# Second block: gate products of the sparse branch issued in pieces between the turns of its attention

## What is computed

```
y_c = dsa_mixer(sq, sk, sv, iq, ik, iw)      # per query block: scores, top-k mask, softmax, weighted values
merged = None
for bi, y in enumerate((y_a, y_b, y_c, y_m)):
    term = jax.nn.sigmoid(u @ w_gate[l, bi]) * (y @ w_branch[l, bi])
    merged = term if merged is None else merged + term
h = h + rms_norm(merged @ w_out[l], norm_mix_post[l])
```

## Time and profile before

| quantity | value |
|---|---|
| median of 3 runs | 2868.74 us |
| profiled execution, its span | 2871.6 us |
| TensorE busy | 2789.8 us (97%) |
| VectorE, ScalarE, POOL busy | 1569.8, 1021.7, 1234.4 us |
| share of the chain that ended last: TensorE | 86% |
| DMA, mean | 68 GB/s |
| attention stage (TensorE) | 1899 to 1983.6 us of the span |
| merge of branch c | 1983.6 to 2093.3 us |

### The profile page before, as it was taken

How to read it: one execution, slowest core, us unless ns; L and a number is a source line. 1 busy time by engine, 2 the same in 40 slices (tenths; PEclk the granted TensorE clock), 3 DMA queues, 4 the chain that set the end, 5 groups by cost and what they waited for, 6 DMA issues and landing times.

```text
span 2871.6 us, 41163 instructions
## 1 busy us (share of the span) xinstructions
PE 2789.8 (97%) x15095; PEld 2247.1 (78%) x15095; DVE 1569.8 (55%) x2437; ACT 1021.7 (36%) x1680; POOL 1234.4 (43%) x960
## 2 busy tenths in 40 slices
PE   7999989999999999999998999989999999999998
PEld 5788778887888887788777888866878888888886
DVE  6444431126255246544488999974156665555655
ACT  4444542333233344333354222144344222222223
POOL 1434312237788641222321343311413766766664
PEclk9999999999999999999999999999999999999999
DMA  6111021213321451211110111100141112112114
GB/s 235 48 34 41 19 89 47 94 59 106 110 59 44 139 212 67 57 36 42 49 32 27 48 46 50 48 25 12 47 174 66 44 44 66 44 44 66 44 60 145
DMA packets 236591, 195.13 MB, mean 68 GB/s; under 512 B 24068, under 2 KB 218301, under 8 KB 232509
## 3 DMA queue, kind: packets, MB, share of 16 engines
q1 hardware_dynamic: 235389, 189.39, 20.7%
q10 hardware_dynamic: 1088, 4.19, 0.4%
HBM read 169.37 MB, written 24.18 MB: 67 GB/s over the span
## 4 chain that ended last, share of the span: by engine, by line
PE 86%; DVE 7%; ACT 2%; issue 2%; POOL 2%; DMA 1%; POOLq 0%; DVEq 0%; ACTq 0%; SPq 0%
PE ps L372 38%; PE ps L4527 13%; PE ps L1684 9%; PE ps L2256 5%; PE ps L1989 3%; PE ps L4477 2%; PE ps L4478 2%; PE ps L4479 2%; PE ps L1095 1%; PE ps L1109 1%; DVE score L3624 1%; PE ps L707 1%; PE ps L3959 1%; DMA x_tok<-in_x 1%; PE ps L3970 1%
## 5 line engine op out<-in xcount | busy, mean ns | idle before, releaser
L355 POOL TENSOR_TENSOR w_lo<-raw,w_hi 128x512 fp32r<-128x512 f32 (+2 forms) x278 | 312.6, 1147 | 741.5 <-ACT w_hi L347 741.5
L372 PE MATMUL ps<-h_hi,w_hi 128*128 128x512 f32 x1472 | 584.5, 397 | 0.0
L372 PE MATMUL ps<-h_hi,w_lo 128*128 128x512 f32 x1472 | 573.8, 390 | 0.0
L372 PE MATMUL ps<-h_lo,w_hi 128*128 128x512 f32 x1472 | 573.5, 390 | 0.0
L372 PEld LDWEIGHTS ps<-h_hi,w_lo 128*128 128x128 f32 x1472 | 276.3, 188 | 59.1
L372 PEld LDWEIGHTS ps<-h_hi,w_hi 128*128 128x128 f32 x1472 | 276.3, 188 | 58.8 <-issue 2.1
L372 PEld LDWEIGHTS ps<-h_lo,w_hi 128*128 128x128 f32 x1472 | 276.6, 188 | 55.8 <-issue 0.5
L347 ACT ACTIVATE w_hi<-raw 128x512 fp32r<-128x512 f32 (+2 forms) x280 | 135.9, 534 | 450.5 <-PE ps L372 439.8
L4380 DVE TENSOR_TENSOR acc<-acc,ps 128x1024 f32<-128x1024 f32 x144 | 169.2, 1213 | 5.7
L3725 DVE MATCH_REPLACE8 score<-best,score 128x384 f32<-128x384 f32 (+2 forms) x192 | 165.8, 876 | 0.0
L3726 DVE MAX8 best<-score 128x8 f32<-128x384 f32 (+2 forms) x192 | 155.7, 878 | 1.1
(11 more groups left out here) (575 smaller groups left out, 6217.6 us busy)
## 6 DMA issues: line engine op xcount, KB each, us to landing
raw<-in_w_in SPq DMA_DIRECT2D x86, 512.0 KB, 3.9
raw<-in_w_ffn_gate_up SPq DMA_DIRECT2D x44, 512.0 KB, 4.8
raw<-in_w_gate SPq DMA_DIRECT2D x32, 512.0 KB, 3.9
d_raw<-in_w_ffn_down SPq DMA_DIRECT2D x20, 512.0 KB, 5.5
acc_pair<-acc_kept SPq DMA_DIRECT2D x8, 1024.0 KB, 4.9
x_kept<-acc SPq DMA_DIRECT2D x16, 512.0 KB, 2.6
acc_kept<-acc_pair SPq DMA_DIRECT2D x7, 1024.0 KB, 3.9
w_ada<-in_w_ada SPq DMA_DIRECT2D x6, 1024.0 KB, 12.7
```

The costliest lines, as they stand in the source:

```text
L355: pool.tensor_tensor(w_lo[:, to, cut], raw[:, s, cut], w_hi[:, to, cut].bitcast(F32), ALU.subtract).then_inc(split.sem, 1)
L372: last = pe.matmul(dst, w[:, slot, k], x(k), start=(k == ks[0] and n == 0), stop=(k == ks[-1] and n == 2))
```

## The change

The 8 gate chunks of branch c move into the attention. A chunk's 48 matmuls are cut into 4 pieces of 12, which makes 32 pieces: two stand between the first scores, the other 30 one behind each turn, except behind turns 5, 11, 17, 23, 29 and 35 of 0 to 35. Two pieces fill one bank (the upper half of `ps[3]`) with half a tile, 512 tokens; ACT then copies it into `acc` (`copy_gate`), and the next half waits for that copy. So `acc` holds the raw gates, and the running sum of the other branches is stored to HBM before (`sum_before`, four stores of 1 MB: three in the first merge, one early in the attention). The attention's result keeps the other half of `ps[3]` only, so the first weigh of block n now waits for the result of block n-1. VectorE's `rest_o` is moved ahead of the next block's `bias_scores`. Behind the attention `merge_kept` takes the place of the merge: SP loads the sum back (4 MB) into the space of `h_lo` once the last gate product has been made, and behind these loads come the branch chunks 2 to 7; ACT makes the Sigmoids in place, TensorE the 96 branch matmuls, VectorE multiplies and adds. Nothing of the computation is left out.

```diff
-        def merge(acc, branches, accumulate, following, beside=None, early=None, residual_gate=None, gate_row=None):
+        def merge(acc, branches, accumulate, following, beside=None, early=None, residual_gate=None, gate_row=None, kept=None):
...
+                    if kept is None:
+                        stream(sp, N, per, merge_source(branches), following,
+                               wide_loads if early or residual_gate is not None else None)
+                    else:
+                        source = merge_source(branches)
+                        for i in range(N):
+                            for m in range(2, per + 2):
+                                if i and m == 6:
+                                    sp.wait_ge(o_evicted.sem, o_evicted.at(0, i, len(adds)))
+                                    sp.wait_ge(sum_kept.sem, sum_kept.at(i - 1))
+                                    tiles_done = slice(KT - 2 * i, KT - 2 * i + 2)
+                                    sp.dma_start(kept[:, tiles_done], acc[:, tiles_done]).then_inc(sum_kept.sem, 16)
+                                load_chunk(sp, m, i, per, source(i, m) if m < per else source(i + 1, m - per) if i + 1 < N else
+                                           following(0, m - per))
...
-            gates, tile_added = ended["gates"], ended["tiles"]
+            gates, tile_added, h_used = ended["gates"], ended["tiles"], ended["h_used"]
...
-                    sum_high(act, rows, acc, tile_added)
+                    sum_high(act, rows, acc, tile_added, h_used)
...
-            return chunk_of(w_in2, m * P + S_Q)
-
-        def sparse_attention(y_hi_t, y_lo_t, score, kv_t, following):
+            return chunk_of(w_in2, m * P + S_Q) if m < 2 else chunk_of(w_gate2[2], ROW_ORDER[m - 2] * P)
+
+        def sparse_attention(y_hi_t, y_lo_t, score, kv_t, acc, kept, following):
...
+            PER = 2 + KT
+            PIECES = 4
+            EARLY_PIECES = 2
...
-                    c = n % 2 * HALF + half * 2 * P
+                    c = n % 2 * 2 * P
                     return ps[3][half * 64:half * 64 + 64, c:c + 2 * P].rearrange("p (t c) -> p t c", c=P)
+
+                def gate_bank():
+                    return ps[3][:, HALF:]
+
+                filled = [x for x in range(len(turns)) if x % 6 != 5]
+
+                def piece_of(x):
+
+                    return EARLY_PIECES + filled.index(x) if x in filled else None
...
                 @block.sync
                 def _(sp):
-                    stream(sp, 1, 2, sparse_source, following)
-
-                gates, terms, added = ended["gates"], ended["terms"], ended["sums"]
+                    for m in range(2, PER + 2):
+                        load_chunk(sp, m, 0, PER, sparse_source(0, m) if m < PER else following(0, m - PER))
+                        if m == 3:
+                            sp.wait_ge(*added)
+                            sp.wait_ge(sum_kept.sem, sum_kept.at(KT // 2 - 1))
+                            sp.dma_start(kept[:, 0:2], acc[:, 0:2]).then_inc(sum_kept.sem, 16)
...
-                    for m in range(2):
-                        rest_chunk(pool, m + 1, 0, 2)
+                    for m in range(PER):
+                        rest_chunk(pool, m + 1, 0, PER, KT if m + 1 < PER else BW // P)
...
+                    def copy_gate(piece):
+                        if piece is None or piece % 2 == 0:
+                            return
+                        n, half = piece // PIECES, piece % PIECES // 2
+                        if half == 0:
+                            act.wait_ge(half_made.sem, half_made.at(n + 1))
+                            if n % 2 == 0:
+                                act.wait_ge(sum_kept.sem, sum_kept.at(n // 2 + 1))
+                        else:
+                            act.wait_ge(used.sem, after(used, 2 + n, 0, PER))
+                        act.activation(acc[:, ROW_ORDER[n], half * HALF:half * HALF + HALF], gate_bank(), ACT.Copy).then_inc(half_copied.sem, 1)
+                        if half:
+                            round_chunk(act, n + 4, 0, PER, KT if n + 4 < PER else BW // P) if n + 4 <= PER else None
+
+                    round_chunk(act, 3, 0, PER)
                     for h in range(H):
                         exps(0, h)
+                        if h % 2 and h // 2 < EARLY_PIECES:
+                            copy_gate(h // 2)
...
+                            if j < b:
+                                copy_gate(piece_of(x))
                         for h in heads:
                             exps(n + 1, h)
+                        copy_gate(piece_of(turns.index((n, b))))
...
                     for n in range(0, TT, 2):
                         normalise(n)
+                        if n >= 1:
+                            rest_o(n - 1)
                         bias_scores(n + 1, (0, 1))
                         bias_scores(n + 1, (2, 3))
-                        if n >= 1:
-                            rest_o(n - 1)
                         normalise(n + 1)
+                        rest_o(n)
                         if n + 2 < TT:
                             bias_scores(n + 2, (0, 1))
-                        rest_o(n)
-                        if n + 2 < TT:
                             bias_scores(n + 2, (2, 3))
                     rest_o(TT - 1)
...
+                    def gate_piece(piece):
+
+                        if piece is None:
+                            return
+                        n, part = piece // PIECES, piece % PIECES
+                        if part == 0:
+                            split_ready(pe, 2 + n, 0, PER)
+                        if part % 2 == 0:
+                            pe.wait_ge(half_copied.sem, half_copied.at(piece // 2))
+                        outs = [(gate_bank(), hi, lo) for _, hi, lo in wide(ps[3])]
+                        last = product(pe, (2 + n, 0, PER), outs, part=(part, PIECES))
+                        if part == 1:
+                            last.then_inc(half_made.sem, 1)
+                        elif part == 3:
+                            last.then_inc(used.sem, 1)
...
-                            pe.wait_ge(o_evicted.sem, o_evicted.at(n - 1))
+                            pe.wait_ge(o_evicted.sem, o_evicted.at(n))
                         for half in range(2):
                             rows, c = slice(half * DH, half * DH + DH), half * 2 * P
-                            last = pe.matmul(ps[3][rows, n % 2 * HALF + c:n % 2 * HALF + c + 2 * P], v_two[:, j, half],
+                            last = pe.matmul(ps[3][rows, n % 2 * 2 * P:n % 2 * 2 * P + 2 * P], v_two[:, j, half],
...
                     score_heads(0, 0)
+                    gate_piece(0)
                     score_heads(0, 2)
+                    gate_piece(1)
                     pe.wait_ge(aux3.sem, aux3.at(3))
                     score_heads(1, 0)
...
                                 weigh(n, j - 1)
                             if j == (0 if small else min(2, order[n])) and n + 1 < TT:
                                 score_heads(n + 1, 2)
+                            gate_piece(piece_of(turns.index((n, j))))
                         if not small and n + 2 < TT:
                             score_heads(n + 2, 0)
                         weigh(n, order[n])
...
+        def kept_source(i, m):
+            return chunk_of(w_branch2[2], ROW_ORDER[m] * P)
+
+        def merge_kept(acc, kept, y_hi_t, y_lo_t, following):
+
+            K2 = BW // P
+            back = h_lo[:].bitcast(F32)
+            y_done = ended["y"]
+            h_used = used.sem, after(used, -1, 0, KT)
+
+            @block.sync
+            def _(sp):
+                sp.wait_ge(*h_used)
+                sp.wait_ge(sum_kept.sem, sum_kept.at(KT // 2))
+                for n in range(KT // 2):
+                    at = ROW_ORDER[2 * n]
+                    sp.dma_start(back[:, at:at + 2], kept[:, at:at + 2]).then_inc(xt_loaded[n].sem, 16)
+                stream(sp, 1, KT, kept_source, following)
+
+            @block.gpsimd
+            def _(pool):
+                for m in range(1, KT + 1):
+                    rest_chunk(pool, m, 0, KT, K2 if m < KT else KT)
+
+            @block.scalar
+            def _(act):
+                for n in range(KT):
+                    tile = acc[:, ROW_ORDER[n]]
+                    act.wait_ge(half_copied.sem, half_copied.at(2 * n + 2))
+                    act.activation(tile, tile, ACT.Sigmoid).then_inc(tile_gated.sem, 1)
+                    round_chunk(act, n + 1, 0, KT, K2 if n + 1 < KT else KT)
+
+            @block.vector
+            def _(dve):
+                for n in range(KT):
+                    tile = acc[:, ROW_ORDER[n]]
+                    dve.wait_ge(tile_gated.sem, tile_gated.at(n + 1))
+                    dve.wait_ge(used.sem, after(used, n, 0, KT))
+                    dve.tensor_tensor(tile, tile, ps[n % 4][:], ALU.mult).then_inc(tile_weighed.sem, 1)
```

(26 more changed lines are left out.)

38 lines of the change are left out of this document (26 added, 12 removed).

## The result

The changed kernel takes 2879.9 us (median of 5 runs, 2876.6 to 2880.7) where the kernel before takes 2868.7: a ratio of 1.0037, 95% interval 1.0026 to 1.0048, **slower by 11.1 us**. A second comparison of the same two kernels gave 1.0027 (1.0017 to 1.0038), which is 8.5 us. The forecast was 2873.6 us with a range of 2860 to 2885: the time is inside the range, 6.3 us above the forecast, and on the other side of the 0.2% line, a case that had a chance of 0.41.

The account below looks back on a forecast made before the run. No engine bounds the attention, with 23.8 us of standing and half clock; matmuls fill the merge. Attention 168.6, merge 30.2 and projection 0.4 make 199.2 against 194.3 us: + 4.9, so 2873.6 us, range 2860 to 2885.

Parts of the forecast that it names:

- Three stands for the bias: Attention: TensorE waits for VectorE's next bias, behind rest_o, after three big blocks; 7.0 us in all.
- Block n=3's first weigh: Attention: TensorE waits for block n-1's rest, which VectorE makes after 4.03 us of normalisation; 2.5 us.
- Switching: Attention: changing between pieces and other matmuls costs 0.22 us for each of 32 pieces; 7.0 us.
- the 60.8 + 87.8 of the prediction: Attention: its own TensorE work at full clock, 60.8 us, plus the 384 moved gate matmuls, 87.8 us.
- Clock in the attention: Attention: one fall to half clock behind the new stands, 1.7 us; ends none, 0, and all four, 6.8 us.
- the clock rival: Attention: the clock falls at every new stand, three falls more, 5.1 us, so 2878.7 us; chance 0.2.
- the other waits: Attention: small waits at blocks n=1, 3, 5 and 7 and before first turns; 1.8 us together.
- The merge: Behind the attention: 22.0 us of matmuls, 1.8 idle, 4.7 standing for chunk 2, 1.7 clock fall; 30.2 us.
- The rival by which the sum's loads hold nothing up: Merge: chunk 2 comes in time, 4.7 + 1.7 us go, so 2867.2 us; chance 0.15.
- The projection: Its first matmul waits 1.22 us for the last multiplication, partly offset by earlier roundings; 0.4 us added.
- The sequencer rival: Attention: pieces hide the 12.2 us of issue gaps at turns and weighs; if all, 2861.4 us; chance 0.2.
- idle time of 23.8 us: Attention before the change: 84.6 us less 60.8 of own work, standing and half clock; the most filling can win.

Follow-up runs that it names:

- e1: Changed kernel with branch chunk 2 issued ahead of the kept sum's four loads, which then go singly between the chunks: 2871.6 us, 1.0003 of the kernel before.
- e2: Changed kernel with VectorE's rest_o put after the bias of the next block's first two heads, not before it: 2870.2 us, 0.9994 of the kernel before.
- e3: Changed kernel with VectorE's rest of a small block's output after the first piece of the next block's normalisation, not the last: 2873.7 us, 1.0011 of before.
- e4: Changed kernel with GpSimd splitting gate chunks 6 and 8 only after VectorE's normalisation of block n=3 or n=5: 2875.1 us, 1.0020 of the kernel before.
- e8: e5 with the last piece behind the last weighing, turn 33 empty, chunk 1 rounded before the first Sigmoid, projection waiting for an earlier multiplication: 2852.4 us, 0.9939.
- e10b: The kernel before, unaltered, profiled again: 2868.8 us, ratio 0.9995.
- e0: The changed kernel, unaltered, run again: 2878.5 us, 1.0027 of the kernel before.
- e9: Changed kernel without filling (30 pieces behind the last weighing), with the edits of e1, e2 and e3: 2883.2 us, 1.0047 of the kernel before.
- e5: Changed kernel with all four edits of e1 to e4 together: 2855.4 us, 0.9949 of the kernel before.

## Why the prediction held, and where it did not

The account was right in its places: each new wait that it named is in the trace, and e1, e2 and e3 showed each to be what it was said to be. By its own steps:

- **Three stands for the bias**, forecast 2.3, 2.3 and 2.2 us: 2.30, 2.17 and 2.04. Right, and e2 removes them by undoing the order that the prediction blamed.
- **Block n=3's first weigh**, 2.5 us: 4.72. The mechanism was right, the 4.03 us of normalisation in it were not: beside GpSimd's split they took 6.17. e4 gives 2.57 without that. I had read the row of 4.03 us in a stage where GpSimd did nothing, and the change brings GpSimd's work into it. The Trainium skill (SBUF — State Buffer, section Who interferes with whom) states that a VectorE instruction with two inputs in SBUF contends with a GpSimd instruction that reads SBUF, at a port pair that one of them holds at a time. The trace agrees: both operands of this multiplication are in SBUF, as are those of the split, and side by side they took 6.17 us, near the 4.03 + 2.51 of one after the other. The page spoke against taking the 4.03 us over, and I had not weighed it.
- **Switching**, 7.0 us: about 2. The 0.21 us a piece are there, but the turn behind a piece is 0.15 shorter. e8's attention, at full clock throughout, confirms it: 149.5 us to its last weighing, less 1.5 of stands, plus the piece that stands outside, 2.75, is 150.8 us; the 60.8 + 87.8 of the prediction are 148.6. So 2.2 us, 0.07 a piece, if the 60.8, an estimate, is right. The 0.22 a piece read from the earlier trace rows was right for the piece; what the turn behind it gets back I had left out.
- **Clock in the attention**, one fall at 1.7 us: three falls at some 1.4 us, 4.2. This is the clock rival in part (it had four falls at 1.7 us; that its time, 2878.7 us, lies near the measured one does not bear it out, since falls in the attention make only 2.5 us of what was missing), and the point it was to decide from, the granted clock behind each stand, was the right one to look at. The argument from the stand of the earlier trace rows, amid dense products, did not carry over.
- These errors cancel: 5.0 us too much for switching, 0.5 for the bias and 0.6 for the other waits (1.8 forecast, 1.2 found); against them 2.2 too little at n=3, 2.5 for the clock, and 1 us that I cannot assign. That the stage came out at 168.2 for 168.6 is therefore luck in the sum; the places of the stands are not.
- **The merge**, 30.2 us: 32.7. The stand behind the sum's loads was forecast at 4.7 and is 3.70, but the forecast was not too high there. A fall behind the 1.76 us stand, which I had not counted, made products 0 and 1 some 1.6 us longer (they take 4.46 us to the second's start, and 2.90 in e2), and the stand shorter by as much, so this fall costs nothing in the changed kernel. What counts is when chunk 2 was ready, 12.9 us behind the last weighing where the forecast had 12.0: 0.9 us. The half clock behind it, 1.7 in the forecast, lasted from 2078 to some 2085 us. From this stand's end to the projection took 21.45 us, where six products at full clock, 2.80 us each as in e1, and the wait of 1.58 us make 18.4: some 3.1 us for the half clock, 1.4 more than forecast. The six products were forecast at 2.75 us each, which makes the last 0.3. The rival by which the sum's loads hold nothing up is out.
- **The projection**, 0.4 us net: 1.58 us at its first product. What follows is shorter than before, 777.4 us from there to the end against 778.2 (779.8 in e10b), so the net is + 0.8 us against one execution of the kernel before and - 0.8 against the other, and the forecast of 0.4 lies between.
- **The sequencer rival** (2861.4 us) is out: nothing of 10 us is missing in the attention. e8's, without its stands, is 2.2 us longer than 60.8 + 87.8.
- **The base.** The idle time of 23.8 us, from which all gain was reckoned, came from an execution with two falls more than e10b had; there it is 82.1 - 60.8 = 21.3 us. I had set the sum against that execution and then moved it to the median as if nothing in the stages differed. The distance to the median was wrong too: in every run on record the time is some 1.8 us more than the span of its execution, so that the execution with a span of 2871.6 us stood some 4.7 us above the median of 2868.7, and not 2.9. The forecast of the difference, + 4.9 us, does not depend on it.

So the way from the + 4.9 us of the forecast to the + 11.1 measured is: from the attention's start to the end, the changed kernel took 979.9 us, 7.2 more than the execution the prediction was read from (the terms above), and 8.1 more than e10b (the base). Its own second execution, e0, took 10.9 more than e10b, with the falls of its clock at other stands and longer. The two profiled executions, of the kernel before and the changed one, lie only 5.7 us apart, since the changed kernel's reached the attention 1.5 us earlier. The rest of the 11.1 us is that the first stood 4.7 us above the median of its kernel, and the second 0.8 below. So it is a matter of which executions are compared; the start of the attention varies by 2 us among the executions of the changed kernel and its variants, and I have not traced that.

**Where did the gain go?** In the stages the runs give this account, in which each figure is one execution and so is known to 2 or 3 us. Before, 191.9 us (e10b). Taking the merge apart, without filling and in good order, makes 207.7 (e9): + 15.8, of which 10.3 are waits for the one bank of the pieces. The filling takes 27.8 off: 179.9 (e5). The four places where the change put work behind other work add 22.6: 202.5. Singly they were 6.5 us for the order of four loads (e1), 9.4 for the place of one call on VectorE (e2), 4 to 5 at block n=3 (e3, e4). With these put right the change is 0.51% faster than the kernel before (e5), and with the merge's start covered 0.61% (e8).

## What to carry to other kernels

Filling one engine's gaps moves every step that the fillers need past work of the other engines: list for each call that changed its place who waits for it, and give the waiting engine its input first, for one misplaced 0.86 us step cost three stands of over 2 us. Durations read in a stage where an engine sleeps do not hold once the change wakes it. When transfers of 1 MB and of 128 KB share a queue, issue the small one that is needed first ahead of them.

## What the hardware showed that I had not expected

- **Whether the clock falls behind a stand of 1.5 to 2.6 us differs from execution to execution of the same code.** Behind the 2.30 us stand it fell in the changed kernel's first profile and not in its second (e0); behind the 2.04 us stand it was the other way round; behind the 1.76 us stand at the merge's start it fell in e5 and not in e2 or in e5's second execution; behind the 2.44 us stand it fell in one execution of the kernel before and not in the other. Behind 0.34 to 0.60 us (e5, e8) it never fell. A fall cost 1.4 us amid pieces (two cases), 1.6 us over the merge's first two products, and some 3.1 us behind the 3.70 us stand. So a stand is best priced at its length plus a share of 1.4 us. The falls seem to make up a good part of the scatter between runs: of e0's eight the fastest, 2873.6 us, has a mean granted clock of 0.994, and the slowest, 2881.2 us, has 0.991. What decides whether a given stand is followed by a fall, no run here shows.
- **VectorE and GpSimd slow each other** when both read two operands from SBUF: 4.03 to 6.17 us and 2.51 to 3.72 us. With one operand in PSUM VectorE was not slowed, though GpSimd was at work, and the sum of two SBUF tiles right before it was (1.75 instead of 1.23 us):

```profile
2096.95 1.75 DVE L4125 TENSOR_TENSOR acc<-acc,h_lo 128x1024 f32<-128x1024 f32 x1
2098.63 1.21 DVE L4122 TENSOR_TENSOR acc<-acc,ps 128x1024 f32<-128x1024 f32 x1
```

```profile
2096.33 3.52 POOL L361 TENSOR_TENSOR w_lo<-raw,w_hi 128x512 fp32r<-128x512 f32 x2 [2.24 <-ACT w_hi L353]
```

- A turn of four transposes takes 0.44 us behind a piece and 0.59 us behind a weighing, so that work of another kind between them is nearly free.
